# Delta rule of both directions taken through each stage together, in a two-layer hybrid mixer kernel

## The reference

```
def gated_delta_chunkwise(q, k, v, g, beta, s0):
    ...
    gcs = jnp.cumsum(g, axis=-1)
    decay = jnp.exp(jnp.where(incl, gcs[..., :, None] - gcs[..., None, :], -jnp.inf))
    kb = k * beta[..., None]
    a_mat = jnp.where(strict, jnp.einsum('bnhid,bnhjd->bnhij', kb, k) * decay, 0.0)
    ...
    sol = lax.linalg.triangular_solve(a_mat + jnp.eye(GDN_CHUNK, dtype=a_mat.dtype), rhs, ...)
    u, w = sol[..., :dv], sol[..., dv:]
    attn = jnp.einsum('bnhid,bnhjd->bnhij', q, k) * decay
    ...
    def step(s, inp):
        u_n, w_n, qd_n, kd_n, at_n, dec_n = inp
        v_new = u_n - jnp.einsum('bhcd,bhde->bhce', w_n, s)
        o = jnp.einsum('bhcd,bhde->bhce', qd_n, s) + jnp.einsum('bhij,bhje->bhie', at_n, v_new)
        s = s * dec_n[..., None, None] + jnp.einsum('bhcd,bhce->bhde', kd_n, v_new)
        return s, o
```

## Time and profile before

| | us |
|---|---|
| median of 3 runs (lowest, highest) | 2384.67 (2384.08, 2387.81) |
| profiled execution, its own time | 2387.21 |
| its span, first to last instruction | 2385.4 |
| PE busy (share of the span) | 2222.8 (93%) |
| DVE busy | 486.9 (20%) |
| ACT busy | 339.8 (14%) |
| POOL busy | 346.8 (15%) |
| mean granted TensorE clock | 0.962 |

### The profile page before, as it was taken

One profiled execution on the slowest core, in us unless ns is written; L12 is line 12 of the kernel. 1 busy time (PEld: TensorE's weight loads), 2 busy tenths in 40 slices (PEclk: granted clock), 3 DMA queues, 4 the chain that ended last, 5 costly groups with the idle time before them and its releaser, 6 DMA issues. The chain is left out here.

```text
span 2385.4 us, 59257 instructions
## 1 busy us (share of the span) xinstructions
PE 2222.8 (93%) x27351; PEld 1374.4 (58%) x27351; DVE 486.9 (20%) x1187; ACT 339.8 (14%) x747; POOL 346.8 (15%) x361
## 2 busy tenths in 40 slices
PE   6998888999999999999789799999999999999985
PEld 3544576644444444466588566666666667676743
DVE  2134444421000100215545420100010101000012
ACT  3105331101000000211532210000000000000001
POOL 1914153000000000094354000000000000000000
PEclk9999999999999999999999799999999999999987
DMA  8322354471222102022000399999889998989895
GB/s 303 106 71 103 130 194 143 143 246 36 92 85 71 53 0 71 19 101 76 1 3 3 140 355 378 377 403 407 294 304 385 336 388 336 387 308 300 285 358 225
DMA packets 173043, 478.12 MB, mean 200 GB/s; under 512 B 11018, under 2 KB 35962, under 8 KB 172666
## 3 DMA queue, kind: packets, MB, share of 16 engines
q1 hardware_dynamic: 170064, 473.95, 54.3%
q10 hardware_dynamic: 2730, 0.34, 0.1%
HBM read 473.21 MB, written 1.05 MB: 199 GB/s over the span
## 5 line engine op out<-in xcount | busy, mean ns | idle before, releaser
L564 PE MATMUL bank<-ring,hT 128*32 128x256 f32 (+2 forms) x12032 | 624.1, 355 | 22.2 <-issue 11.5
L564 PE MATMUL bank<-hT,ring 128*128 128x512 f32 (+1 forms) x1568 | 629.1, 560 | 10.2 <-ACT hT L1295 6.7
L564 PEld LDWEIGHTS bank<-ring,hT 128*32 128x32 f32 (+1 forms) x12032 | 406.5, 112 | 230.0 <-issue 30.1
L564 PEld LDWEIGHTS bank<-hT,ring 128*128 128x128 f32 x1568 | 299.7, 194 | 325.0 <-issue 308.0
L564 PE MATMUL bank<-ring,gates 128*32 128x256 f32 x5152 | 292.4, 384 | 10.4 <-DMA ring<-in_moe_w_dram 10.0
L564 PEld LDWEIGHTS bank<-ring,gates 128*32 128x32 f32 x5152 | 181.5, 111 | 112.6 <-DMA ring<-in_moe_w_dram 13.9
L564 PE MATMUL bank<-ring 64*64 64x64 f32 (+2 forms) x4672 | 209.1, 240 | 27.2 <-ACT ring L1295 15.9
L564 PEld LDWEIGHTS bank<-ring 64*64 64x64 f32 (+2 forms) x4672 | 171.9, 139 | 56.1 <-issue 39.2
L2230 DVE TENSOR_TENSOR gates<-gates,bank 128x512 f32<-128x512 f32 (+3 forms) x50 | 27.6, 581 | 666.6 <-PE bank L564 666.6
L1295 ACT ACTIVATE gates<-bank 128x512 f32<-128x512 f32 (+3 forms) x108 | 48.8, 514 | 801.5 <-PE bank L567 608.5
L564 PE MATMUL bank<-work,ring 128*128 128x512 f32 x352 | 151.5, 593 | 2.3 <-DVE work L2021 1.4
(11 more groups left out here) (192 smaller groups left out, 1237.0 us busy)
## 6 DMA issues: line engine op xcount, KB each, us to landing
ring<-in_moe_w_dram SPq DMA_DIRECT2D x336, 1024.0 KB, 7.5
ring<-in_ada_w_dram SPq DMA_DIRECT2D x24, 2048.0 KB, 8.2
ring<-in_ffn_w_dram SPq DMA_DIRECT2D x23, 1024.0 KB, 8.0
ring<-in_w_in_dram SPq DMA_DIRECT2D x10, 2048.0 KB, 8.1
ring<-in_ffn_w_dram SPq DMA_DIRECT2D x5, 2048.0 KB, 7.9
ring<-in_w_out_dram SPq DMA_DIRECT2D x4, 2048.0 KB, 8.1
ring<-in_w_in_dram SPq DMA_DIRECT2D x2, 1024.0 KB, 11.3
table<-const_table SPq DMA_DIRECT2D x1, 1890.0 KB, 11.9
```

The lines of the kernel that those rows point to most:

```text
L564: return nc.tensor.matmul(o, w, x, start=start, stop=stop)
```

## The change

`delta(l, d)` becomes `delta(l)`, called once a layer. Every stage loops over `BOTH`, the eight pairs of tile and direction, and a step of the loop takes step n of both directions. The two directions get buffers of their own: the arena is carved in two halves of 10240 columns, keys turned share the place of the inverse, `gW` and `gU` take over `gP1` and `gNT`, and states and new values of both directions lie side by side. The scalings for direction 1 (`kbqd1`) go from POOL to DVE (`beta_keys`). Those for direction 0 no longer wait until all four tiles are ready. The right-hand sides are made after levels 1 to 4 instead of before level 3, the scaled keys `gKD` after the levels. `between` does in layer 0 one half of an ada product in each part (two a joint step), in layer 1 three matmuls in each part (six a joint step). The output of a step of direction d gathers in one bank (6 + d), both head pairs, and is read by one DVE operation of 256 columns instead of two of 128. Small products in the loop rotate over 5 banks in layer 0 (the same five as before) and 4 in layer 1 (before 6). `ada_turn(1, 1)`, which stood between the two directions, now stands after step 4 of the loop.

The core of the diff:

```diff
-        gTB, gAA, gKQ, gW, gU, gP1, gNT, gKD, gRW, gRU, gKB = carve(arena, (2048,) * 3 + (1024,) * 8)
+        GDIR = 10240
+        gTB, gQ, gAA, gNT, gP1, gKD, gRW, gRU = zip(*(
+            carve(arena, (2048, 1024, 2048, 1024, 1024, 1024, 1024, 1024)) for _ in range(2)))
+        gW, gU = gP1, gNT
...
+        BOTH = [(t, d) for t in range(TT) for d in range(2)]
...
+            def between(l, n, part):
+                if l == 0:
+                    ada(1)
                     return
+                ks = (0, 1, 4, 5, 6, 7)[3 * part:3 * part + 3]
...
-            def delta(l, d):
+            def delta(l):
                 R6 = range(6)
+                RS = range(4) if l else range(5)
...
-                for t in range(TT):
+                for t, d in BOTH:
                     key = ("kq", l, d, t)
-                    pe.wait_ge(*when("kbqd", (l, d, t)))
+                    pe.wait_ge(*when(f"kbqd{d}", (l, t)))
...
                 for v in range(1, 6):
-                    for t in range(TT):
+                    for t, d in BOTH:
                         pe.wait_ge(*when("NT", (l, d, v, t)))
...
+                for n in range(8):
+                    at_step = [steps(d)[n] for d in range(2)]
+                    for d, (t, c) in enumerate(at_step):
+                        cs = CHUNKS[c]
+                        key = ("vn", l, d, n)
+                        pe.wait_ge(*drained(("w", l, d, c)))
+                        if n:
+                            pe.wait_ge(*drained(("su", l, d, n - 1)))
+                        o = product(key, RS)
...
+                    between(l, n, 0)
+                    for d, (t, c) in enumerate(at_step):
+                        if l and t < 2:
+                            continue
...
+                            mm(psum[6 + d][:, at:at + CHUNK], states[:, d, i, :],
+                               grp(gQ[d], t, 256)[:, at:at + CHUNK], i == 0, False)
+                    for d, (t, c) in enumerate(at_step):
+                        cs = CHUNKS[c]
+                        pe.wait_ge(*when("kd", (l, d, t)))
+                        pe.wait_ge(*drained(("vn", l, d, n)))
+                        key = ("su", l, d, n)
+                        o = product(key, RS)
...
+                    between(l, n, 1)
+                    if (l, n) == (0, 4):
+                        ada_turn(1, 1)
...
+            def delta(l):
+                def beta_keys(t):
+                    at = 16 + 4 * t
+                    if t >= 2:
+                        dve.wait_ge(*full(("kq", l, 1, t - 2)))
+                    dve.wait_ge(*when("qk_unit", (l, t)))
+                    step(scaled(kbuf(1, t)[:, 0:256], tok[:, t, 256:512], beta, at))
+                    scaled(kbuf(1, t)[:, 256:512], tok[:, t, 0:256], gex, at).then_inc(*mark("kbqd1", (l, t)))
+                beta_keys(0)
+                beta_keys(1)
...
                 pool.wait_ge(*when("decays", l))
                 for t in range(TT):
                     pool.wait_ge(*when("qk_unit", (l, t)))
                     if t >= 2:
-                        pool.wait_ge(*full(("kq", l, d, t - 2)))
...
+                        pool.wait_ge(*full(("kq", l, 0, t - 2)))
```

More of the change, by code:

```diff
@@ L1920, in delta @@
                         .then_inc(*read(key))
-                for t in range(TT):
+                    if d and t < 2:
+                        beta_keys(t + 2)
+                for t, d in BOTH:
                     dve.wait_ge(*when("decay_ready", (l, d, t)))
@@ L2050, in _ @@
                     ada(0, 2)
-                delta(l, 0)
-                if l == 0:
-                    ada(1, 1)
-                delta(l, 1)
+                delta(l)
                 delta_finish(l)
```

394 lines of the change are left out of this document (193 added, 201 removed).

## The result

| | before | after |
|---|---|---|
| median of six runs (lowest, highest), us | 2384.12 (2380.95, 2387.81) | 2364.49 (2358.72, 2370.35) |
| span of the profiled execution | 2385.4 | 2363.7 |
| the two delta stages, together | 310.33 | 287.37 |

The ratio is 0.9917, with a 95% interval of 0.9897 to 0.9936: 19.6 us faster, where 19.0 were forecast. The medians and the profiles don't give quite the same gain: in the profiled executions the delta stages alone shrank by 23.0 us and the whole span by 21.7. A delta stage is counted here from DVE's first scaling of queries and keys (L1910, now L1934) to the first product of the head norm behind the loop.

What follows compares the result with a forecast made beforehand. PE was taken as nearly filled, in balance with DVE's chain in the loop. Gains of 6.8 us in layer 0 and 12.2 in layer 1, together 19.0, from the median 2384.7 gave 2365.7 us; range 2354 to 2379, about 0.8.

Steps and rivals of the forecast that it cites:

- Both signs of being wrong: Prediction wrong if layer 1 gains no more than layer 0, or delta stretches shrink while time outside them grows.
- Outside the stages: Rest of the program: nothing changes, so gains in the delta stretches pass to the end in full.
- Loop, layer 0: Joint steps of 5.9, later 6.4 us set by weight slots; 51.0 against 54.1 us, gain 3.1.
- Loop, layer 1: Joint steps of 5.3, then 6.8 us; 48.8 against 54.05 us, gain 5.2, of which 3 from 1.2 GHz ending.
- Levels: Eight tiles every 11.2 us, PE filled; gains 1.8 and 2.2 us from half-clock stretches coming once instead of twice.
- Between levels and loop: Stretch from levels to loop, both directions together: 8.4 us in layer 0, 7.5 in layer 1; gains 1.8 and 1.5.
- Fronts: Joint fronts of 27.8 us in layer 0 and 25.5 in layer 1; gains 0.9 and 3.5.
- POOL's early start: In the front, POOL's reads beside DVE's last tile scalings delay the turns; 0.5 us lost a layer.
- Locks: Rival: DVE and POOL block each other in the front, 1.20 us per DVE operation; 2370.8 us, chance 0.12.
- The slower rival: In joint loop steps PE stands through DVE's second set of updates, 1.22 us more each; 2393.5 us, chance 0.06.
- the forecast's argument against it: In the loop, ada or residual products and `go` already lie behind `su`, covering 1.8 us or more, longer than one set.

Runs made afterwards that it cites:

- the stages apart: Changed kernel with nothing joint: fronts, levels, w/u, then loops, each one direction after the other; 2376.84 us, ratio 0.9968, 300.13 us in the delta stages.
- the late start of POOL: Changed kernel with POOL's first scalings waiting until DVE has scaled all four tiles, as before the change; 2362.92 us, ratio 0.9898.

## Why the prediction was right, point by point

The time was right, and the closeness is in part luck. Between the two profiles the stages shrank by 23.0 us where the sum had 19.0, and the terms were off both ways. Both signs of being wrong stayed away: layer 1 gained more than layer 0 (14.1 and 8.8 us in the stages, 12.2 and 6.8 forecast), and the time outside grew by 1.2 us only, less than it varies between the profiles.

- **Outside the stages** nothing changed: the two long stretches take 731.5 and 1042.5 us, before 732.7 and 1041.2.
- **Loop, layer 0**: forecast 51.0, measured 49.5. The step was "2 x (0.56 + 0.62 + 0.25 + 0.36) + 2 x 1.06 = 5.70"; PE's part is 4.88. Doubling the times of one direction was wrong, most of all for `su` and `go`, as the two loops of layer 1 show. The second `vn` waits 0.62, not 0.2. The weights were taken to set 6.4 us a step; PE waited for them four times, 2.9 us in all, and the mean step was 5.8 without `ada_turn`.
- **Loop, layer 1**: forecast 48.8, measured 45.75, with 5.1 and 5.9 us a step instead of 5.3 and 6.8. The same term was mis-sized, and so were the six output matmuls, 3.0 us where 3.4 were forecast.
- **Levels**: 55.9 and 53.7 forecast, 55.3 and 54.8 measured, a level of eight tiles every 11.2 to 11.7. They are bound by PE as said, and the 2.3 and 1.1 us gained are not pairing: with the directions apart, levels and w and u together took 64.2 and 63.7 us, joint 64.4 and 63.6. Clock and stalls fit, as forecast.
- **Between levels and loop**: 8.4 and 7.5 forecast, 9.1 and 8.9 measured. Direction 1's `w` and `u` need banks that ACT has yet to copy, and PE waits 1.76 us in the middle in layer 0 and 1.27 in layer 1. The forecast had this wait only behind the last product.
- **Fronts**: 27.8 and 25.5 forecast, 26.5 and 24.3 measured. The first four moved scalings took 0.57 each (2.26 in four), not 0.88, and the turn waited 0.53 for them, not 1.3. `TT_first` was 0.83 each in a row of eight.
- **POOL's early start**: 0.5 us in each layer forecast, 0.8 in layer 0 and 0.1 in layer 1 measured. In this profile layer 0 lost another 0.4 ahead of the first turn, where the clock was 0.57 from 309 to 313 us (1.00 in the stages apart).
- **Locks** didn't cost what the rival had: 0.57 us for a scaling and 0.83 for `TT_first` beside POOL, where that case had 1.20. The two engines did slow each other, as the late start of POOL shows.
- **The slower rival** was real as a mechanism and is switched on by where the filling work stands; the forecast's argument against it was right.
- **What the forecast didn't see**: it counted half-clock stretches that go (3 us in layer 1's loop, the levels' gains) as a result of pairing. 10.2 us come without anything joint, from the new order of the stages and what goes with it. Nor did it see that the second direction's `su` and `go` come nearly free. The errors of the terms (loops 4.6 too little, fronts 2.5 too little, w and u 2.1 too much) partly cancelled.

## What to carry to other kernels

When two independent chains are put together on an engine, ask what happens to the work itself, not only to the waits. Here two directions in opposite halves of the partitions did their state updates in 0.28 us where one took 0.25, and a joined group of output matmuls saved 0.27 us. Splitting like work to fill a hole cost what the hole did. So look which partitions two products read and write before you double their time. Then ask for each gap which work stands in it, since the same joint loop without work behind the updates gave all of the gain back. And test the order of stages by itself before crediting the pairing.

## What the runs showed of the hardware

- PE stalls without a releaser, 1.7 to 3.2 us, when a 2 MB load fills the DMA engines (share 1.04) beside dense small matmuls, 33 records in a microsecond. The changed kernel has one of 1.25 us in its first level, just behind the front's load (share 1.07). Beside the sparser work of the loop the same loads show no such stall.
- Sixteen matmul records of 64x64 took 0.23 us in the front, 0.28 in the joint loop and 0.49 in the levels, all at clock 1.00. The combinations of partition halves that they read and write differ, and four of them in use go with the short times.
- After PE had stood idle for 2.0 to 3.7 us in the loop, the next stretch was granted 1.2 GHz for a part or all of it: 2.44 to 3.56 us for work of 1.92. Shorter waits give no rule: waits of 1.1 us in the changed kernel's loop were followed by full clock (1.06 us for a half), but with the scalings on POOL a half took 1.94 behind a wait of 1.18, and with work between the two `vn` one took 1.85 behind 0.59.
- POOL beside DVE stretched four scalings of 128x512 from 2.50 to 3.33 us, and its own four of 128x256 from 2.33 to 3.50.
